# Large weight buffers and scratch moved down in SBUF, constants and activations moved up, in a two-block network on one core

## What is computed

```python
def first_block(x, ...):
    for l in range(2):
        h = rmsnorm(x, g_mix[l]); z = h @ w_in[l]
        # short convolution, gated spatial mixing, sparse attention, long convolution
        x = x + concat(y_a, y_b, y_c, y_d) @ w_out[l]
        hf = rmsnorm(x, g_ffn[l])
        x = x + (silu(hf @ w_gate[l]) * (hf @ w_up[l])) @ w_down[l]      # hidden width 2816
    return rmsnorm(x, g_final)

def second_block(x, ...):
    x = x + sincos_2d(rows, GRID_W)
    # modulation from c, mLSTM in both directions, Fourier mixing, w_out
    # router: two of four experts in the best of four groups
    for e in range(16):
        a = silu(h @ w_gate[e]) * (h @ w_up[e])
        y = y + combine[..., e, None] * (a @ w_down[e])
    return x + gate2 * rmsnorm(y, g_post_ffn)
```

## Time and profile before

| | |
|---|---|
| median of three runs | 1081.52 us (1081.04 to 1081.78) |
| the profiled execution | 1078.93 us |
| its span in the trace | 1077.2 us |
| TensorE busy | 996.4 us, 92% of the span |
| VectorE, ScalarE, GpSimd busy | 643.3, 379.9, 71.4 us |
| moved by DMA | 251.85 MB, mean 234 GB/s |

### The profile page before, as it was taken

The page is one execution under the profiler, slowest core; times in us unless marked ns, Lnnn a source line. Parts: engine busy times, 40 slices in busy tenths (PEclk is TensorE's granted clock), DMA queues, the critical chain, the costliest instruction groups (busy, mean ns, idle before and its releaser), DMA issues.

```text
span 1077.2 us, 14406 instructions
## 1 busy us (share of the span) xinstructions
PE 996.4 (92%) x5708; PEld 772.2 (72%) x5708; DVE 643.3 (60%) x1270; ACT 379.9 (35%) x590; POOL 71.4 (7%) x111
## 2 busy tenths in 40 slices
PE   5999989999999999989999998999966889999985
PEld 5867779999999867779999997956756334444432
DVE  5798579898765698478898657334647511111112
ACT  5233534433433143534444337246332221111111
POOL 0202000000000002000100001001810000000000
PEclk9999989999996999999999998999985999999998
DMA  9624275675535424187786573022029799999994
GB/s 368 248 81 158 86 301 225 247 282 222 197 149 195 157 79 186 60 340 280 305 351 272 195 293 131 1 78 78 2 95 412 312 410 408 357 385 399 421 422 164
DMA packets 30151, 251.85 MB, mean 234 GB/s; under 512 B 3857, under 2 KB 3985, under 8 KB 5649
## 3 DMA queue, kind: packets, MB, share of 16 engines
q1 hardware_dynamic: 30096, 251.14, 58.9%
HBM read 250.08 MB, written 1.05 MB: 233 GB/s over the span
## 4 chain that ended last, share of the span: by engine, by line
PE 87%; DVE 4%; DMA 3%; ACT 3%; issue 2%; POOL 1%; SPq 0%; DVEq 0%; POOLq 0%
PE bank L674 17%; PE bank L676 17%; PE bank L675 17%; PE bank L665 10%; PE bank L1220 10%; PE bank L1236 6%; DMA blocks_w<-in_experts 2%; PE bank L1197 1%; PE bank L1179 1%; PE bank L689 1%; DMA m<-in_w_in 1%; PE bank L1031 1%; PE bank L712 1%; ACT m L1549 1%; ACT scratch L1603 0%
## 5 line engine op out<-in xcount | busy, mean ns | idle before, releaser
L674 PE MATMUL bank<-h_h,fw_h 128*128 128x256 f32 x704 | 197.0, 280 | 7.4 <-issue 7.4
L676 PE MATMUL bank<-h_h,fw_l 128*128 128x256 f32 x704 | 196.5, 279 | 0.0
L675 PE MATMUL bank<-h_l,fw_h 128*128 128x256 f32 x704 | 196.4, 279 | 0.0
L1929 DVE TENSOR_TENSOR fw_l<-blocks_w,fw_h 128x1024 fp32r<-128x1024 f32 x132 | 156.2, 1218 | 4.3 <-ACT fw_h L1413 4.3
L674 PEld LDWEIGHTS bank<-h_h,fw_h 128*128 128x128 f32 x704 | 134.0, 190 | 9.7 <-issue 8.0
L675 PEld LDWEIGHTS bank<-h_l,fw_h 128*128 128x128 f32 x704 | 134.1, 190 | 1.7
L676 PEld LDWEIGHTS bank<-h_h,fw_l 128*128 128x128 f32 x704 | 133.9, 190 | 0.0
L1413 ACT ACTIVATE fw_h<-blocks_w 128x1024 fp32r<-128x1024 f32 x132 | 129.8, 1051 | 5.5 <-DMA blocks_w<-in_ffn 5.5
L1220 PE MATMUL bank<-m,scratch 128*64 128x512 f32 (+1 forms) x352 | 98.5, 594 | 2.8 <-DMA m<-in_experts 2.8
L1972 DVE SCALAR_TENSOR_TENSOR m<-m,scratch 128x512 f32<-128x512 f32 x128 | 90.1, 745 | 0.0
L1439 ACT ACTIVATE acts<-bank 128x256 f32<-128x256 f32 x44 | 16.9, 385 | 203.3 <-PE bank L676 203.3
(11 more groups left out here) (388 smaller groups left out, 1829.2 us busy)
## 6 DMA issues: line engine op xcount, KB each, us to landing
m<-in_experts SPq DMA_DIRECT2D x56, 1024.0 KB, 11.0
blocks_w<-in_ffn SPq DMA_DIRECT2D x22, 2048.0 KB, 7.9
blocks_w<-in_experts SPq DMA_DIRECT2D x40, 1024.0 KB, 11.4
m<-in_w_ada SPq DMA_DIRECT2D x24, 1024.0 KB, 8.2
m<-in_w_in SPq DMA_DIRECT2D x11, 2048.0 KB, 9.5
blocks_w<-in_ffn SPq DMA_DIRECT2D x22, 1024.0 KB, 4.8
m<-in_w_out SPq DMA_DIRECT2D x6, 2048.0 KB, 7.4
blocks_w<-in_w_in SPq DMA_DIRECT2D x2, 2048.0 KB, 20.3
```

The lines of the kernel that those rows point to most:

```text
L674: pe.matmul(out_, xh, wh, start=first and i == 0, stop=False, skip_group_check=True)
L675: pe.matmul(out_, xh, wl, start=False, stop=False, skip_group_check=True)
L676: ins = pe.matmul(out_, xl, wh, start=False, stop=last and i == n - 1, skip_group_check=True)
L1929: dve.tensor_tensor(fw_l[:, slot, at], blocks_w[:, slot, at], f32(fw_h[:, 1 - slot, at]), ALU.subtract)\
```

## The change

Two `sb` calls move. `kwi_w` is placed first, and `scratch` directly behind `m` instead of last.

```diff
+        kwi_w = sb("kwi_w", [P, KD, 68])
         blocks_w = sb("blocks_w", [P, 2, BLOCK])
         m = sb("m", [P, 4, 4096])
-        kwi_w = sb("kwi_w", [P, KD, 68])
+        scratch = sb("scratch", [P, N_SCRATCH])
         const = sb("const", [P, N_CONST])
         prm = sb("prm", [P, N_PRM])
         prm2 = sb("prm2", [P, N_PRM2])
@@
         half = sb("half", [P, 8])
-        scratch = sb("scratch", [P, N_SCRATCH])
```

## The result

The changed kernel took **1078.27 us**, median of 22 runs (1076.35 to 1082.53), beside 1080.68 us for the kernel before in the same comparison (22 runs, 1078.07 to 1084.66). The ratio is **0.9976, 95% interval 0.9965 to 0.9987**: 2.4 us less by the medians, 1.4 to 3.8 us by the interval. Of the 3.2 us between forecast and result, 0.8 is the level (the kernel before, 1081.52 us in three runs, is 1080.68 in these), and 2.4 is the change.

A forecast was written before the change was run, and what follows sets the result against it. The prediction took TensorE to bound the kernel, with transfers setting the time only at the end of the experts. All terms were 0, so the 1081.52 us median gave a forecast of 1081.5 us, range 1078.5 to 1084.0.

The forecast's parts named there:

- What bounds the kernel: Whole kernel: TensorE is busy 92% of the span; transfers set the time only at the end of the experts.
- TensorE, feed-forward: I take 0: Gate, up and down matmuls in the loop: speed does not depend on operand addresses, 0 us, bounds -2.4 and +10.3.
- The price named for a gain: Gate and up chains: all at 113 ns from their start, 12 × 4.5 ns × 44 chains, 2.4 us less.
- the four pairs of wide matmuls: Wide float32 matmuls with operands in four different pairs of regions, 592 to 596 ns, cited as evidence for no address effect.
- The slow chain outside the loop: Chain with weights in m, 117.9 ns between starts; taken for the +10.3 us bound if every loop chain ran so.
- DMA: I take 0: Ring slots in m and blocks_w becoming aligned: rate unchanged at 426 GB/s, 0 us, bound 1.3 us in either direction.
- VectorE, ScalarE, small tiles: 0: Lines 1929 and 1413 change by 0.1 and 0.7 us at most, covered by TensorE; small tiles keep their remainder; 0 us.
- The first: Rival: aligned ring slots drain the last 80 us of the experts 1.3 us sooner, 1080.2 us; chance 0.10.
- the second: Rival: weight load and moving operand stop interfering in gate and up chains, -2.4 us, 1079.1 us; chance 0.08.
- The third: Rival: weight load and moving operand start interfering in the loop's gate and up chains, 1091.8 us; chance 0.07.
- no duration depends on these addresses: The forecast itself, whole kernel: unchanged at 1081.5 us, given the remaining chance of 0.68.
- The test named for the first rival: Ring at the end: a rate above 430 GB/s with waits near 2 us would prove the alignment rival.

The follow-up runs named there:

- e3: Against the kernel before: blocks_w and m on multiples of 256 at other addresses and in another order, scratch unmoved; 1077.52 us, ratio 0.9987.
- e5: Changed kernel with blocks_w and m beginning 32 bytes off a multiple of 256; 1096.38 us, ratio to before 1.0131.
- e6: Changed kernel with 64 bytes of padding behind const, so x and acts also start on multiples of 256; 1089.31 us, ratio to before 1.0066.
- e9: Changed kernel with a pad of 32 floats behind const, acts at distance 64 from both weights; 1088.55 us, ratio to before 1.0074.
- e15: Changed kernel with a pad of 40 floats behind const, acts at distance 96 from both weights; 1097.33 us, ratio to before 1.0142.
- c2: e1 once more, unedited; 1079.17 us in its one run.
- e1: Kernel before with only kwi_w placed first, which takes blocks_w and m to multiples of 256; 1077.32 us, ratio 0.9973.
- e8: e3 with blocks_w again 128 bytes off a multiple of 256, m on one; 1079.96 us, ratio to before 0.9979.
- e11: Changed kernel with 64 bytes of padding behind kwi_w: weight buffers at remainder 64, acts at 0, distance still 192; 1079.81 us, ratio to before 0.9972.
- e16: Changed kernel with m 128 bytes off a multiple of 256 and blocks_w on one; 1080.72 us, ratio to before 0.9987.
- e2: Kernel before with only scratch moved, blocks_w and m still 128 bytes off a multiple of 256; 1079.84 us, ratio 0.9994.
- e4: Changed kernel's order with blocks_w and m pushed back to 128 bytes off a multiple of 256; 1080.76 us, ratio to before 1.0006.
- e7: Changed kernel with all large buffers sorted onto multiples of 512 bytes; 1088.96 us, ratio to before 1.0066.
- c1: The changed kernel once more, unedited; 1077.88 us, ratio to before 0.9979.

## Why the prediction was wrong

**What bounds the kernel** held: TensorE's spacing in the loop and the drain of the ring at the end are two of the three places where the time changed. For the third, the projections, the sum had no term at all: a term put at nothing without a reason, and 2.1 us in the profiled executions.

**"TensorE, feed-forward: I take 0" failed**; it was -2.0 us, inside the bounds of -2.4 and +10.3. The price named for a gain, 2.4 us if the slow start went away, came near by luck: the slow start only shortened, which gives 42 × 0.026 = 1.1 us, and the other 42 × 0.020 = 0.8 came from the down matmuls, which the bound leaves out. Two of its readings did not carry it. It compared 280 with 279 ns across `fw_h` and `fw_l`, but these rows have the same values in the changed kernel: the change of 26 ns in 48 matmuls is 0.5 ns each, below what a row prints, and still 1.1 us over 2112 of them. And it took the four pairs of wide matmuls as evidence; those are plain float32, and plain float32 is not touched. Line 665 starts its matmuls 429 ns apart with weights in `m` and 216 with weights in `blocks_w`, in before, after, e3, e5, e6 and e9 alike. It did read starts, in the earlier trace rows, and saw 117.5 and then 113 ns. It put the difference down to the position in the chain, since the buffers are the same. But how long the slow start lasts, 12 matmuls or 5, depends on the distance, and e5 to e15 show spacings of up to 8.567 us a step from the same instructions. The slow chain outside the loop was set aside for the same reason, as a matter of position. It had both its weights in `m`, at distance 64, and e9, with both weights at 64, runs at 117.8 ns through all of gate and up in the loop. At distance 192 that very chain ran at 117.8 again in after, but at 113.3 in c2, e1, e8 and e11. A pair of buffers at one pair of distances cannot show what another pair of distances does.

**"DMA: I take 0" failed**; it was -1.4 us against the bound of 1.3. The two rows of 426 GB/s were a lone short transfer and a stretch of only 12 us; over 50 us the rates are 421 and 427. The very next 20 us of the trace before already showed it, busy time by stretch:

```profile
880.00:900.00 20.00, 17.91 (x70) 8.79 (x71) 2.34 (x9) 5.85 (x9) 0.00 (x0) 1.00 1.01 422
```

The changed kernel has 426 there. The 1.3 us had been worked out rightly, and put in the range instead of the sum. The Trainium skill's rule (page "DMA: Bandwidth & Descriptors", section "How a descriptor splits into AXI transactions") gave an estimate of 1.6% for 128 bytes off; the sustained rates differ by 1.4%. So it came near for the case before, but e8 and e16, each with one of two buffers 128 off and 426 and 425 GB/s, do not follow it, nor can it tell that 64 off costs the same as 128 (e11) and 32 off more (e5, 419).

**VectorE, ScalarE, small tiles: 0** held. Line 1929 went from 1218 to 1219 ns. Line 1712, changed kernel, groups by line and shape:

```profile
L1712 DVE TENSOR_TENSOR w_l<-m,w_l 128x1024 fp32r<-128x1024 f32 x24 | 28.5, 1225 | 0.4 <-ACT w_l L1332 0.4
```

8 ns more than in the earlier trace rows, 24 × 8 ns = 0.2 us, covered.

**The rivals.** The first (aligned slots, -1.3 us, chance 0.10) and the second (-2.4 us, chance 0.08) both came true in direction, with 1.4 and 2.0 us. The second blamed `acts` against `scratch`; `scratch` and `acts` keep their distance in the change, e2 moves `scratch` and nothing happens, and it is `fw_l` in `blocks_w` whose distance changed. Its argument against itself, that the same buffers run at 113 ns a microsecond later, was the step that failed: the loop gained by reaching 113 ns after 5 matmuls where it had taken 12. Together they were put at 1077.8 us, which is 3.7 below the forecast; the chance for both was treated as negligible, though both hung on one fact, that the time can depend on addresses, and so belonged together. The third, slower through the same mechanism, did not happen here, but its mechanism is real: the seven other distances in the table, and e5, cost 6 to 15 us by their ratios, around its 10.3. The chance of 0.68 for "no duration depends on these addresses" was the true mistake. **The test named for the first rival** (over 430 GB/s) was set wrong: 427 was enough. The bound of the forecast itself, wrong below 1079.4 us, was crossed.

## What to carry to other kernels

Where TensorE streams without a gap, the placement of its two operands is a tuning parameter: keep the buffers' distance modulo 256 fixed while other things are changed, and try several distances when the rest is settled, since "align everything" cost 0.7% here and the best distance was 192. Judge it by the distance between starts over many repetitions: the mean duration moves too, but here by less than the nanosecond that a row prints. Only the matmuls on rounded operands showed the effect; those on plain float32 did not. Take a DMA rate from the longest saturated stretch. A change that only moves addresses has unknown costs of both signs and deserves no high chance of "no change" unless the trace holds the very same pair of distances.

## What the runs showed of the hardware

- The same 60 matmuls take 8.213 to 8.567 us, 4.3% apart, by the distances modulo 256 between `acts` and the two weight buffers (e5, e6, e9 to e15, after). Other absolute addresses with the same distances give the same steps: 8.213 in e3, e11 and e16, 8.260 in e2, e4 and e8, 8.500 in e6 and e7. The Trainium skill, page "SBUF — State Buffer", section "Who interferes with whom", gives TensorE two independent read ports, one for the moving operand and one for the weight load, and names a port that TensorE does not use as the only place of contention. Nothing in that table would let a distance between two TensorE operands matter, and in the time of these runs it does. What within the chip makes it so, no run here shows.
- Matmuls on plain float32 (line 665) start 429 ns apart for 512 columns and 216 for 256 at six placements (before, after, e3, e5, e6, e9); only those on rounded operands follow the distance. Why is not shown.
- Outside the loops, 191 distances in the third block take 21.65 to 21.67 us in the eight traces with a weight part at 192, 22.50 with both at 64 (before, e2, e4, e9), and up to 22.92 at other distances (e6).
- At distance 192 the same addresses and instructions run at 8.213 or at 8.420 us a step, settled anew in each loop and each execution (after, c1; e1, c2).
- The sustained rate into a ring of two buffers was 426 to 427 GB/s with both or only `m` on multiples of 256, 425 with only `blocks_w`, 421 with both 64 or 128 off, 419 with both 32 off.
